# Feed-forward gate and up layers by seven block products instead of eight, from the third pair on, with every remainder taken on GpSimd

## The chip, the core and the metric

The kernel runs on one core of one Trainium2 chip. The metric is device time in microseconds (us), the median of three runs. Only this core is in use. TensorE (PE in the profile) multiplies, ScalarE (ACT) and VectorE (DVE) do elementwise work and read the matmul results out of PSUM, GpSimd (POOL) does elementwise work between SBUF tiles, and SyncE (SP) issues the weight loads.

## What is computed

Four blocks of a network in float32 over a sequence of 512 tokens of width 1024: two layers of mixer, cross attention and feed-forward, then a block with two more mixers and a feed-forward, then a block of three mixers. Three feed-forward layers are in it, all of the same size; the change touches only them.

```python
def _swiglu(h, w_in, w_out):
    a, g = jnp.split(h @ w_in, 2, axis=-1)
    return (jax.nn.silu(a) * g) @ w_out
...
        x = x + _swiglu(_rmsnorm(x, norm_ffn[l]), ffn_w_in[l], ffn_w_out[l])
```

`w_in` has 1024 rows and 2 x 2816 columns, so gate and up are 22 column blocks of 128 each. The first two layers (f0 and f1 below) normalise by a root mean square; the third (fs) has separate gate and up weights and a layer norm ahead of it.

## The kernel before

Activations are kept transposed: 128 partitions are 128 features, the 512 columns are the tokens, and the width of 1024 is 8 tiles. A float32 product is made of three passes of the fast matmul format: each operand is split into a rounded part (high, `XH`, `WH`) and a remainder (low, `XL`, `WL`), and `unit_passes` (L274 to L276) multiplies high by high, high by low and low by high into one PSUM bank.

Weights arrive as a stream of 527 units of 128 x 1024, in an order written out by hand. Each unit passes a pipeline: SP loads it into one of 4 buffers `RW`; ACT rounds it into one of 3 buffers `WH` (`w_hi`, L269), as soon as PE has finished the unit three before; POOL subtracts to get `WL` (L3351); PE multiplies it. One unit of a gate or up layer is one block of 128 output features over all 1024 inputs: 8 weight blocks x 3 passes = 24 matmuls of 512 columns.

The gate and up layer is the class `Pairs`: unit 2i is the gate block i, unit 2i+1 the up block i. PE writes the two into two of four PSUM banks. In f0 and f1 the factor of the root-mean-square norm is applied late, on the result (`late`): DVE multiplies both banks by the factor `NR` (L503, `scaled`), ACT applies Silu to the gate (L488), DVE multiplies the two in SBUF (L525). In fs ACT reads the gate bank itself (L483), and one DVE instruction (L525) multiplies it with the up bank. After 22 pairs comes `Down`, which sums the 22 hidden tiles into all 8 banks; its activations are split by ACT (L638) and DVE (L642). At the start of f0 and f1 DVE makes the remainders of the activations (L936) while PE already works, and at the end of the second unit PE sums squares for the factor, whose reciprocal DVE takes (L976).

Each engine's program is written out in advance and runs in order; engines meet at counting semaphores (`split_hi` and `split_done` for rounded weights and their remainders, `unit_done` for a unit that PE has finished).

## Time and profile before

| | |
|---|---|
| median of three runs | 3389.99 us (3388.49 to 3391.5) |
| profiled execution, first to last instruction | 3388.5 us |
| TensorE's mean granted clock | 0.990 of full speed |
| busy: PE, PEld | 3283.3 us (97%), 2632.3 us (78%) |
| busy: DVE, ACT, POOL | 1319.2, 1220.6, 1331.1 us (39%, 36%, 39%) |
| chain that ended last | PE 86%, DVE 7%, ACT 2% |

The profiled execution lies 1.5 us under the median of the runs. PE is a matmul, PEld its weight load, which overlaps the matmul before it. A matmul's duration in the trace includes its way through the array, so the distance between two starts, not the duration, says what one costs in a row of them.

### The profile page before, as it was taken

The page shows a single profiled execution, that of the slowest core. Times are in us where ns is not written, and L with a number is a line of the kernel's source. Part 1 is how long each engine was busy: PE and PEld are TensorE (multiplying, and loading weights), DVE is VectorE, ACT ScalarE, POOL GpSimd, SP SyncE. Part 2 cuts the span into 40 slices and gives each one's busy share as a digit, 9 for nine tenths or more (in the row PEclk, how much of TensorE's full clock was granted, in tenths as well). Part 3 has the DMA queues.
Part 4 walks back from the last instruction along what each step waited for, and adds up shares of the span by engine and source line. Part 5 has one row for each costly group of instructions (what it writes and reads, how often), then busy time and mean ns, then how long its engine had stood idle before and what let it go on. Part 6 is the DMA issues. An engine that isn't in the chain of part 4 may idle for free.

```text
span 3388.5 us, 41020 instructions
## 1 busy us (share of the span) xinstructions
PE 3283.3 (97%) x17376; PEld 2632.3 (78%) x17376; DVE 1319.2 (39%) x1957; ACT 1220.6 (36%) x1856; POOL 1331.1 (39%) x555
## 2 busy tenths in 40 slices
PE   8999999999999999999999999999899999999998
PEld 6778788887788788886677876888688778878887
DVE  8953421214443421213448652001373261133733
ACT  4543422223343322224434433222335432342332
POOL 5734244443254244443143023444344324415443
PEclk9999999999999999999999999999999999999999
DMA  4222132222232132223123032232232212212332
GB/s 165 87 94 94 50 100 94 99 97 90 69 109 90 56 100 95 98 100 103 49 84 119 19 113 75 99 98 95 81 113 96 72 56 97 90 38 94 100 119 74
DMA packets 83006, 302.48 MB, mean 89 GB/s; under 512 B 9060, under 2 KB 10888, under 8 KB 81928
## 3 DMA queue, kind: packets, MB, share of 16 engines
q1 hardware_dynamic: 78368, 280.55, 25.1%
q10 hardware_dynamic: 4456, 19.33, 1.5%
q8 instruction: 137, 2.24, 0.3%
q14 instruction: 45, 0.37, 0.0%
HBM read 290.39 MB, written 9.44 MB: 88 GB/s over the span
## 4 chain that ended last, share of the span: by engine, by line
PE 86%; DVE 7%; ACT 2%; issue 1%; DVEq 0%; ACTq 0%
PE PS L274 23%; PE PS L276 23%; PE PS L275 23%; PE PS L1197 2%; PE PS L570 2%; PE PS L572 2%; PE PS L571 2%; PE PS L1318 1%; PE PS L2306 1%; DVE XL L936 1%; PE PS L1007 1%; PE PS L2298 1%; PE PS L1183 1%; PE PS L2982 1%; ACT WH L269 0%
## 5 line engine op out<-in xcount | busy, mean ns | idle before, releaser
L3351 POOL TENSOR_TENSOR WL<-RW,WH 128x1024 fp32r<-128x1024 f32 x527 | 1297.3, 2464 | 2029.4 <-ACT WH L269 2028.8
L274 PE MATMUL PS<-XH,WH 128*128 128x512 f32 x2968 | 1169.2, 394 | 33.8 <-DVE XL L936 15.5
L275 PE MATMUL PS<-XL,WH 128*128 128x512 f32 x2968 | 1160.1, 391 | 0.0
L276 PE MATMUL PS<-XH,WL 128*128 128x512 f32 x2968 | 1160.0, 391 | 0.0
L269 ACT ACTIVATE WH<-RW 128x1024 fp32r<-128x1024 f32 x527 | 554.1, 1054 | 802.3 <-PE PS L276 705.7
L274 PEld LDWEIGHTS PS<-XH,WH 128*128 128x128 f32 x2968 | 560.7, 189 | 171.4 <-issue 24.4
L275 PEld LDWEIGHTS PS<-XL,WH 128*128 128x128 f32 x2968 | 560.6, 189 | 117.1 <-issue 2.2
L276 PEld LDWEIGHTS PS<-XH,WL 128*128 128x128 f32 x2968 | 560.2, 189 | 117.4
L274 PE MATMUL PS<-YH,WH 128*128 128x512 f32 (+1 forms) x928 | 349.5, 377 | 7.5 <-DVE A L408 2.9
L276 PE MATMUL PS<-YH,WL 128*128 128x512 f32 (+1 forms) x928 | 348.1, 375 | 0.0
L275 PE MATMUL PS<-YL,WH 128*128 128x512 f32 (+1 forms) x928 | 348.1, 375 | 0.0
L503 DVE TENSOR_TENSOR SG<-PS,NR 128x512 f32<-128x512 f32 x136 | 93.4, 691 | 534.3 <-PE PS L276 533.9
L274 PEld LDWEIGHTS PS<-YH,WH 128*128 128x128 f32 x928 | 175.3, 189 | 42.5 <-POOL WL L3351 6.2
L275 PEld LDWEIGHTS PS<-YL,WH 128*128 128x128 f32 x928 | 175.5, 189 | 31.2
L276 PEld LDWEIGHTS PS<-YH,WL 128*128 128x128 f32 x928 | 175.4, 189 | 31.0
L488 ACT ACTIVATE SG<-SG 128x512 f32<-128x512 f32 x80 | 50.6, 632 | 351.3 <-DVE SG L503 351.2
L642 DVE TENSOR_TENSOR YL<-A,YH 128x512 fp32r<-128x512 f32 x66 | 50.3, 772 | 262.6 <-ACT YH L638 262.6
L408 DVE TENSOR_TENSOR A<-PS,NR 128x512 f32<-128x512 f32 (+1 forms) x84 | 53.3, 638 | 165.1 <-PE PS L276 164.6
L638 ACT ACTIVATE YH<-A 128x512 fp32r<-128x512 f32 x66 | 40.7, 629 | 211.3 <-PE PS L276 211.3
L525 DVE TENSOR_TENSOR A<-SG,PS 128x512 f32<-128x512 f32 x30 | 20.6, 688 | 213.8 <-PE PS L276 202.6
L1241 DVE TENSOR_REDUCE SM<-PS 128x1 f32<-128x256 f32 (+3 forms) x128 | 56.0, 470 | 98.1 <-PE PS L3115 52.2
L1427 DVE SCALAR_TENSOR_TENSOR PS<-A,VEC,PS 128x499 f32<-128x499 f32 (+14 forms) x108 | 79.8, 739 | 4.6 <-ACT A L373 0.8
(549 smaller groups left out, 3089.2 us busy)
## 6 DMA issues: line engine op xcount, KB each, us to landing
RW<-in_units SPq DMA_DIRECT2D x527, 512.0 KB, 3.3
spill<-X ACTq DMA_DIRECT2D x2, 2048.0 KB, 7.5
X<-in_xT SPq DMA_DIRECT2D x8, 256.0 KB, 6.9
A<-spill ACTq DMA_DIRECT2D x1, 2048.0 KB, 8.9
X<-spill ACTq DMA_DIRECT2D x4, 512.0 KB, 5.8
X<-spill ACTq DMA_DIRECT2D x1, 2048.0 KB, 8.6
out_T<-X ACTq DMA_DIRECT2D x4, 512.0 KB, 3.0
spill<-X ACTq DMA_DIRECT2D x1, 1536.0 KB, 5.1
```

What stands on the lines that cost most here:

```text
L269: nc.scalar.activation(WH[:, u % SPLIT, :], RW[:, u % RAW, :], ACT.Copy).then_inc(split_hi, 1)
L274: mm(out, hi, xh, start=first, stop=False)
L275: mm(out, hi, xl, start=False, stop=False)
L276: return mm(out, lo, xh, start=False, stop=last)
L503: st.do(nc.vector.tensor_tensor(dst, bank((e + q) % 4), self.late.r, ALU.mult), name)
L570: mm(o, xh, wh, start=(k == 0), stop=False)
L571: mm(o, xh, wl, start=False, stop=False)
L572: last = mm(o, xl, wh, start=False, stop=(k == KT - 1))
L1197: last = mm(PS[rows, 6 + n % 2, c0:S], value(j), self.pt_of(s, g)[:, j, c0:S], start=(j == 0), stop=(j == (TT if self.keys is None else se ...
L1241: st.do(nc.vector.tensor_reduce(SM[:, c:c + 1], bank(2 * (it % 2) + s, self.blocks_of(it) * P), AX.X, ALU.max, negate=True), f"{self.id}.m ...
L1427: st.do(v.scalar_tensor_tensor(out=y[:, sh:], in0=T(k)[:, :S - sh], scalar=w, in1=y[:, sh:], op0=ALU.mult, op1=ALU.add), f"conv.sum{k}")
L3351: nc.gpsimd.tensor_tensor(WL[:, u % SPLIT, :], RW[:, u % RAW, :], WH[:, u % SPLIT, :].bitcast(F32), ALU.subtract).then_inc(split_done, 1)
```

## The change

From the third pair on, in each of the three layers, the 20 remaining pairs of units are handled by a new class `Sevens`. A pair of units is seen as a 2 x 2 matrix: rows are gate and up, columns are the first and second half of the 1024 inputs. The activations are also seen as 2 x 2: upper and lower half of the inputs by left and right half of the 512 tokens. The eight block products of this 2 x 2 product are replaced by seven (Strassen's method in Winograd's form). Each product has four weight blocks in three passes and 256 columns: 12 matmuls of 256 columns.

The seven left operands (terms, 128 x 512 each) are A11, S1, S2, S4, S3, A12 and A22. Three are halves of the loaded units; the four S are sums of halves, which DVE makes for each pair in advance (`sums`, into `TERM`, `SD`, and S1 over the loaded half itself). Each term is then rounded by ACT (`term_hi`) and its remainder taken by POOL (`pool`). The 3 buffers of `WH` and `WL` become 6 half buffers. Four mixed right operands are made once for each layer (`mix`, `mix_hi`, `mix_lo`), in the time of the first two pairs, which stay as they were. The results are put together in PSUM where it can be done (products S2, S4, S3 and A22 are accumulated onto what stands in a region), and by three copies on ACT and three additions on DVE where it can't.

The counting of the old semaphores is corrected for the units that no longer pass them (`plain`).

```diff
-        A = sb("A", [P, 38, S])
+        with nc.sbuf_tensor("A", [P, 38, S], F32) as A:
+            pass
+        sb("A_LOW", [P, 22, S])
+        MIXED = sb("MIXED", [P, 16, S], F32R)
...
+        def raw_free(eng, u):
+
+            s7 = sevens_of(u)
+            if s7 is None:
+                eng.wait_ge(split_done, plain(u) + 1)
...
+            def gained(self, st, out, half, cols, other, op):
+                if self.gain is None:
+                    st.do(nc.vector.tensor_tensor(out, self.x(half, cols), other, op))
+                else:
+                    for k in range(4):
+                        st.do(nc.vector.scalar_tensor_tensor(out=out[:, k, :], in0=self.x(half, cols)[:, k, :], scalar=vec(self.gain, 4 * half + k),
+                                                             in1=other[:, k, :], op0=ALU.mult, op1=op))
...
+            def mix_hi(self, st, t):
+                st.wait(f"{self.name}.mix{t}")
+                st.do(nc.scalar.activation(self.mixed(t)[0], self.sum_of(t), ACT.Copy), f"{self.name}.mixhi{t}")
+
+            def mix_lo(self, st, t):
+                hi, lo = self.mixed(t)
+                st.wait(f"{self.name}.mixhi{t}")
+                st.do(nc.vector.tensor_tensor(lo, self.sum_of(t), hi.bitcast(F32), ALU.subtract), f"{self.name}.mixed{t}")
+
+            def opening(self, st):
+                for t in range(4):
+                    self.mix(st, t)
+                for t in range(2):
+                    self.mix_lo(st, t)
+
+            def rounded(self, st):
+                for t in range(4):
+                    self.mix_hi(st, t)
+
+            def between(self, st, i):
+                if i == 0:
+                    self.mix_lo(st, 2)
+                    self.sums(st, 0)
+                    self.mix_lo(st, 3)
...
+            def term_hi(self, st, q):
+                p, m = q // 7, q % 7
+                if m in (self.A11, self.A12, self.A22):
+                    raw_landed(st, self.u0 + 2 * p + self.RAWS[m][0])
+                else:
+                    st.wait(f"{self.name}.sum{m}.{p}")
+                if q < 2 * SPLIT:
+                    split_free(st, self.u0 + q // 2)
+                else:
+                    st.wait_ge(product_done, self.base + q - 2 * SPLIT + 1)
+                nc.scalar.activation(WHH[:, self.slot(q), :], self.raw(p, m), ACT.Copy).then_inc(term_hi, 1)
+
+            def pool(self, pool):
+                for q in range(7 * self.n):
+                    w = self.slot(q)
+                    pool.wait_ge(term_hi, self.base + q + 1)
+                    nc.gpsimd.tensor_tensor(WLH[:, w, :], self.raw(q // 7, q % 7), WHH[:, w, :].bitcast(F32), ALU.subtract).then_inc(term_done, 1)
+
+            def sums(self, st, p):
+                a11, a12, a21, a22 = (self.raw(p, m) for m in (self.A11, self.A12, self.S1, self.A22))
+                s2, s3, s4 = (self.raw(p, m) for m in (self.S2, self.S3, self.S4))
+                for w in range(2):
+                    raw_landed(st, self.u0 + 2 * p + w)
+                if p:
+                    st.wait_ge(term_done, self.base + 7 * (p - 1) + self.S3 + 1)
+                st.do(nc.vector.tensor_tensor(s3, a11, a21, ALU.subtract), f"{self.name}.sum{self.S3}.{p}")
+                st.do(nc.vector.scalar_tensor_tensor(out=a21, in0=a21, scalar=-1.0, in1=a22, op0=ALU.mult, op1=ALU.subtract), f"{self.name}.sum{self.S1}.{p}")
+                st.settle()
+                st.do(nc.vector.scalar_tensor_tensor(out=s2, in0=a21, scalar=-1.0, in1=a11, op0=ALU.mult, op1=ALU.subtract), f"{self.name}.sum{self.S2}.{p}")
+                st.settle()
+                st.do(nc.vector.tensor_tensor(s4, a12, s2, ALU.subtract), f"{self.name}.sum{self.S4}.{p}")
...
+                kept = {self.S2: "first", self.S4: "fifth", self.S3: "second", self.A22: "third"}
+                mixes = {self.S1: 0, self.S2: 1, self.S3: 2, self.A22: 3}
+                for p in range(self.n):
+                    for m in range(7):
+                        q = 7 * p + m
+                        st.wait_ge(term_done, self.base + q + 1)
+                        if m == 0:
+                            bank_free(st, self.e0 + 2 * p + 1)
+                        if m in kept:
+                            st.wait(f"{self.name}.{kept[m]}{p}")
+                        if p == 0 and m in mixes:
+                            st.wait(f"{self.name}.mixed{mixes[m]}")
+                        xh, xl = self.operand(m)
+                        for k in range(4):
+                            c = slice(k * P, (k + 1) * P)
+                            last = unit_passes(self.region(p, where[m]), WHH[:, self.slot(q), c], WLH[:, self.slot(q), c], xh[:, k, :], xl[:, k, :],
+                                               k == 0 and m in (self.A11, self.S1, self.A12), k == 3, m in kept)
+                        last.then_inc(product_done, 1)
...
+                    self.done(st, p, 0)
+                    st.do(a.activation(SG[:, j, 0:256], self.region(p, 0), ACT.Copy), f"{self.name}.first{p}")
+                    ahead(0)
+                    self.done(st, p, 1)
+                    st.do(a.activation(SG[:, 2 + j, 256:S], self.region(p, 1), ACT.Copy), f"{self.name}.fifth{p}")
+                    ahead(1)
+                    self.done(st, p, 2)
+                    st.do(a.activation(SG[:, j, 256:S], self.region(p, 0), ACT.Copy), f"{self.name}.second{p}")
+                    for m in range(2, 7):
+                        ahead(m)
+                        if m == 3 and p == self.n - 1:
+                            self.then.lead_act(act, st)
+                    st.wait(f"{self.name}.gated{p}")
+                    st.do(a.activation(SG[:, j, :], SG[:, j, :], self.func), f"{self.name}.func{p}")
...
+                    if p < self.n - 1:
+                        self.sums(st, p + 1)
+                    else:
+                        self.then.lead_dve(dve, st)
+                    self.done(st, p, 3)
+                    st.wait(f"{self.name}.second{p}")
+                    st.do(v_.tensor_tensor(gate[:, right], c, gate[:, right], ALU.add))
+                    self.done(st, p, 4)
+                    st.wait(f"{self.name}.fifth{p}")
+                    st.do(v_.tensor_tensor(up[:, right], a, up[:, right], ALU.add), f"{self.name}.third{p}")
+                    self.done(st, p, 5)
+                    st.wait(f"{self.name}.first{p}")
+                    st.do(v_.tensor_tensor(gate[:, left], b, gate[:, left], ALU.add), f"{self.name}.taken{p}")
+                    st.settle()
+                    if self.late is not None:
+                        st.do(v_.tensor_tensor(gate, gate, self.late.r, ALU.mult), f"{self.name}.gated{p}")
+                        st.do(v_.tensor_tensor(up[:, right], up[:, right], self.late.r[:, right], ALU.mult))
+                    else:
+                        names[f"{self.name}.gated{p}"] = names[f"{self.name}.taken{p}"]
+                    self.done(st, p, 6)
+                    if self.late is not None:
+                        st.do(v_.tensor_tensor(up[:, left], a, self.late.r[:, left], ALU.mult))
+                        st.settle()
+                        st.wait(f"{self.name}.func{p}")
+                        st.do(v_.tensor_tensor(self.dst(self.first + p), gate, up, ALU.mult), f"ev{e + 1}")
+                    else:
+                        st.wait(f"{self.name}.func{p}")
+                        st.do(v_.tensor_tensor(self.dst(self.first + p)[:, left], gate[:, left], a, ALU.mult))
+                        st.do(v_.tensor_tensor(self.dst(self.first + p)[:, right], gate[:, right], up[:, right], ALU.mult), f"ev{e + 1}")
...
-            up = Pairs(f"f{l}.up", NH, at(0), ACT.Silu, ready=f"fn{l}", late=late, first=first)
-            up.then = Down(f"f{l}.down", up, alpha, summed, weights)
-            return up.then
+            up = Pairs(f"f{l}.up", 2, at(0), ACT.Silu, ready=f"fn{l}", late=late, first=first)
+            s7 = up.sevens = Sevens(f"f{l}.up", 2, NH - 2, at(0), ACT.Silu, None if late is None else f"norm_ffn{l}", late, f"fn{l}.biased7")
+            up.opening, up.opening_act, up.rounded, up.between = s7.opening, s7.mix_open_act, s7.rounded, s7.between
+            s7.then = Down(f"f{l}.down", up, alpha, summed, weights)
+            return s7.then
...
+                s7 = sevens_of(u)
+                if s7 is not None:
+                    if u == s7.u0:
+                        s7.pool(pool)
+                    continue
+                pool.wait_ge(split_hi, plain(u) + 1)
```

The instruction order of DVE shows what a pair is made of. This is DVE in f0, before, from the reciprocal of the norm's factor on (names in front of `<-` are written, behind it read; `SG` is the working tile of a pair, `A` on the left of L525 the hidden tile):

```order
L976 RECIPROCAL NR<-NR 128x512
L503 TENSOR_TENSOR SG<-PS,NR 128x512 x2
L525 TENSOR_TENSOR A<-SG 128x512
L503 TENSOR_TENSOR SG<-PS,NR 128x512 x2
L525 TENSOR_TENSOR A<-SG 128x512
```

In the changed kernel the same place reads (L679 are the four mixes in 16 pieces, L711 their remainders, L552 and L576 the old pair, L763 to L768 the sums):

```order
L1251 RECIPROCAL NR<-NR 128x512
L679 SCALAR_TENSOR_TENSOR A<-X,VEC,A 128x256 x16
L711 TENSOR_TENSOR MIXED<-A,MIXED 128x1024 x2
L552 TENSOR_TENSOR SG<-PS,NR 128x512 x2
L576 TENSOR_TENSOR A<-SG 128x512
L711 TENSOR_TENSOR MIXED<-A,MIXED 128x1024
L763 TENSOR_TENSOR TERM<-RW 128x512
L764 SCALAR_TENSOR_TENSOR RW<-RW 128x512
L766 SCALAR_TENSOR_TENSOR SD<-RW 128x512
L768 TENSOR_TENSOR TERM<-RW,SD 128x512
L711 TENSOR_TENSOR MIXED<-A,MIXED 128x1024
```

The mixes and two of their remainders stand ahead of the first pair's own three instructions, and the other two remainders with the first sums ahead of the second pair's. From then on a pair of `Sevens` in f0 and f1 is these eleven DVE instructions (the sums are those of the next pair):

```order
L763 TENSOR_TENSOR TERM<-RW 128x512
L764 SCALAR_TENSOR_TENSOR RW<-RW 128x512
L766 SCALAR_TENSOR_TENSOR SD<-RW 128x512
L768 TENSOR_TENSOR TERM<-RW,SD 128x512
L844 TENSOR_TENSOR SG<-PS,SG 128x256
L847 TENSOR_TENSOR SG<-PS,SG 128x256
L850 TENSOR_TENSOR SG<-PS,SG 128x256
L853 TENSOR_TENSOR SG<-SG,NR 128x512
L854 TENSOR_TENSOR SG<-SG,NR 128x256
L859 TENSOR_TENSOR SG<-PS,NR 128x256
L862 TENSOR_TENSOR A<-SG 128x512
```

Three instructions have become eleven, and the four sums stand ahead of the additions that PE's last product of the pair waits for (L847, named `third`). On POOL the order before ends, after a few taps of a convolution (L1408, L1410) between the first units, in one instruction for each of the other 505 units:

```order
L1410 TENSOR_TENSOR A<-A 128x501 [waits pool_taps]
L3351 TENSOR_TENSOR WL<-RW,WH 128x1024 [waits split_hi]
L1408 TENSOR_SCALAR A<-A,VEC 128x500 [waits pool_taps]
L1410 TENSOR_TENSOR A<-A 128x500 [waits pool_taps]
L3351 TENSOR_TENSOR WL<-RW,WH 128x1024 [waits split_hi] x505
```

and POOL's order in the changed kernel at f0 has the following in its place, seven of half the width for each pair:

```order
L3633 TENSOR_TENSOR WL<-RW,WH 128x1024 [waits split_hi] x46
L754 TENSOR_TENSOR WL<-RW,WH 128x512 [waits term_hi] x2
L754 TENSOR_TENSOR WL<-SD,WH 128x512 [waits term_hi]
L754 TENSOR_TENSOR WL<-TERM,WH 128x512 [waits term_hi] x2
L754 TENSOR_TENSOR WL<-RW,WH 128x512 [waits term_hi] x4
L754 TENSOR_TENSOR WL<-SD,WH 128x512 [waits term_hi]
```

Two instructions of 1024 columns for each pair have become seven of 512.

## Rows read from the trace of the kernel before

**Rows 1.** The page, part 1: busy time, share, instructions of each engine

```profile
PE 3283.3 (97%) x17376; PEld 2632.3 (78%) x17376; DVE 1319.2 (39%) x1957; ACT 1220.6 (36%) x1856; POOL 1331.1 (39%) x555
```

**Rows 2.** Busy time in stretches of f0 and fs, then clock, DMA share

```profile
440.00:640.00 200.00, 200.00 (x884) 165.68 (x883) 38.67 (x56) 48.65 (x55) 90.48 (x38) 1.00 0.30 99
2100.00:2300.00 200.00, 200.00 (x884) 165.68 (x883) 12.38 (x18) 48.48 (x56) 86.91 (x37) 1.00 0.30 98
```

**Rows 3.** Timeline of DVE in f0: start, duration, engine, line, what, idle before

```profile
499.77 0.69 DVE L503 TENSOR_TENSOR SG<-PS,NR 128x512 f32<-128x512 f32 x1 [4.02 <-PE PS L276]
505.21 0.69 DVE L503 TENSOR_TENSOR SG<-PS,NR 128x512 f32<-128x512 f32 x1 [4.75 <-PE PS L276]
505.94 0.69 DVE L525 TENSOR_TENSOR A<-SG 128x512 f32<-128x512 f32 x1
510.65 0.69 DVE L503 TENSOR_TENSOR SG<-PS,NR 128x512 f32<-128x512 f32 x1 [4.02 <-PE PS L276]
```

**Rows 4.** Timelines of ACT and POOL at the same place of f0

```profile
500.50 0.63 ACT L488 ACTIVATE SG<-SG 128x512 f32<-128x512 f32 x1 [5.04 <-DVE SG L503]
501.03 1.04 ACT L269 ACTIVATE WH<-RW 128x1024 fp32r<-128x1024 f32 x1
...
502.15 2.40 POOL L3351 TENSOR_TENSOR WL<-RW,WH 128x1024 fp32r<-128x1024 f32 x1 [4.16 <-ACT WH L269]
506.41 2.47 POOL L3351 TENSOR_TENSOR WL<-RW,WH 128x1024 fp32r<-128x1024 f32 x1 [1.85 <-ACT WH L269]
```

**Rows 5.** Timeline of PE in the memory keys, 21 steps of 256 columns

```profile
156.26 0.28 PE L276 MATMUL PS<-YH,WL 128*128 128x256 f32 x1
...
158.78 0.28 PE L276 MATMUL PS<-YH,WL 128*128 128x256 f32 x1
```

**Rows 6.** Timeline of POOL, 501 beside 1024 columns, and two in a row

```profile
127.89 1.27 POOL L1410 TENSOR_TENSOR A<-A 128x501 f32<-128x501 f32 x1
129.12 2.40 POOL L3351 TENSOR_TENSOR WL<-RW,WH 128x1024 fp32r<-128x1024 f32 x1
...
435.69 4.76 POOL L3351 TENSOR_TENSOR WL<-RW,WH 128x1024 fp32r<-128x1024 f32 x2 [9.06 <-ACT WH L269]
```

**Rows 7.** Timelines of POOL and DVE where both have work in a row

```profile
962.00 26.86 POOL L3351 TENSOR_TENSOR WL<-RW,WH 128x1024 fp32r<-128x1024 f32 x10 [1.41 <-ACT WH L269]
...
962.47 2.49 DVE L895 TENSOR_TENSOR XL<-A,XH 128x512 fp32r<-128x512 f32 x1 [0.44 <-ACT XH L1852]
964.88 0.41 DVE L408 TENSOR_TENSOR A<-PS,NR 128x256 f32<-128x256 f32 x1
965.22 2.56 DVE L895 TENSOR_TENSOR XL<-A,XH 128x512 fp32r<-128x512 f32 x1
...
979.31 2.56 DVE L895 TENSOR_TENSOR XL<-A,XH 128x512 fp32r<-128x512 f32 x1
```

**Rows 8.** Timeline of DVE at the start of f0; last row, 2048 columns

```profile
413.91 4.38 DVE L936 SCALAR_TENSOR_TENSOR XL<-X,VEC,XH 128x512 fp32r<-128x512 f32 x4 [0.87 <-ACT XH L926]
...
418.80 2.74 DVE L936 SCALAR_TENSOR_TENSOR XL<-X,VEC,XH 128x512 fp32r<-128x512 f32 x4
...
429.81 3.35 DVE L976 RECIPROCAL NR<-NR 128x512 f32<-128x512 f32 x1 [5.44 <-ACT NR L968]
...
439.93 0.69 DVE L503 TENSOR_TENSOR SG<-PS,NR 128x512 f32<-128x512 f32 x1 [3.88 <-PE PS L276]
...
147.48 2.28 DVE L1514 TENSOR_TENSOR A<-A 128x2048 f32<-128x2048 f32 x1
```

**Rows 9.** Timeline of DVE at the end of f0's pairs

```profile
654.95 4.28 DVE L642 TENSOR_TENSOR YL<-A,YH 128x512 fp32r<-128x512 f32 x4 [2.17 <-ACT YH L638]
...
659.87 2.17 DVE L525 TENSOR_TENSOR A<-SG 128x512 f32<-128x512 f32 x1
```

**Rows 10.** Timeline of DVE at the start of fs

```profile
2080.45 0.69 DVE L895 TENSOR_TENSOR XL<-X,XH 128x512 fp32r<-128x512 f32 x1 [0.59 <-ACT XH L1054]
2086.80 0.69 DVE L525 TENSOR_TENSOR A<-SG,PS 128x512 f32<-128x512 f32 x1 [5.65 <-ACT SG L483]
```

More of the change, by code:

```diff
@@ L260, in bank_free, with sevens_of, plain, raw_landed @@
                 st.wait_ge(*reached(f"ev{e - 4}"))
+        SEVENS = []
+        def sevens_of(u):
+            for s7 in SEVENS:
+                if s7.u0 <= u < s7.u0 + 2 * s7.n:
+                    return s7
+            return None
+        def plain(u):
+            return u - sum(min(max(u - s7.u0, 0), 2 * s7.n) for s7 in SEVENS)
+        def raw_landed(st, u):
+            st.wait_ge(raw_full[u % RAW], 16 * (u // RAW + 1))
+        def raw_free(eng, u):
[3 more added lines that the diff above has]
+            else:
+                eng.wait_ge(term_done, s7.base + 7 * ((u - s7.u0) // 2) + 6 + (u - s7.u0) % 2)
+        def split_free(st, u):
+            if u >= SPLIT:
+                s7 = sevens_of(u - SPLIT)
+                if s7 is None:
+                    st.wait_ge(unit_done, plain(u - SPLIT) + 1)
+                else:
+                    st.wait_ge(product_done, s7.base + 7 * s7.n - 6 + 2 * (u - s7.u0 - 2 * s7.n + 1))
         def w_hi(act, st, v):
@@ L265, in w_hi, with unit_passes @@
                 u = st.unit
-                st.wait_ge(raw_full[u % RAW], 16 * (u // RAW + 1))
-                if u >= SPLIT:
-                    st.wait_ge(unit_done, u - SPLIT + 1)
-                nc.scalar.activation(WH[:, u % SPLIT, :], RW[:, u % RAW, :], ACT.Copy).then_inc(split_hi, 1)
+                s7 = sevens_of(u)
+                if s7 is not None:
+                    if u - s7.u0 >= SPLIT:
+                        return
+                    for q in range(2):
+                        s7.term_hi(st, 2 * (u - s7.u0) + q)
+                else:
+                    raw_landed(st, u)
+                    split_free(st, u)
+                    nc.scalar.activation(WH[:, u % SPLIT, :], RW[:, u % RAW, :], ACT.Copy).then_inc(split_hi, 1)
                 st.unit = u + 1
-        def unit_passes(out, hi, lo, xh, xl, first, last):
-            mm(out, hi, xh, start=first, stop=False)
-            mm(out, hi, xl, start=False, stop=False)
-            return mm(out, lo, xh, start=False, stop=last)
+        def unit_passes(out, hi, lo, xh, xl, first, last, onto=False):
+            mm(out, hi, xh, start=first, stop=False, skip_group_check=onto)
+            mm(out, hi, xl, start=False, stop=False, skip_group_check=onto)
+            return mm(out, lo, xh, start=False, stop=last, skip_group_check=onto)
         def pe_tile(pe, st, u, e, xh, xl, cols):
-            st.wait_ge(split_done, u + 1)
+            st.wait_ge(split_done, plain(u + 1))
             bank_free(st, e)
@@ L440, in __init__ @@
             def __init__(self, name, n, dst, func, of=0, yh=None, acc=False, ready=None, u_off=0, func2=None, late=None, first=1,
-                         between=None, between_act=None, between_pe=None, eager=0):
+                         between=None, between_act=None, between_pe=None, eager=0, opening=None, opening_act=None, rounded=None):
                 self.eager, self.held = eager, False
+                self.opening, self.opening_act, self.rounded = opening, opening_act, rounded
                 self.between, self.between_act, self.between_pe = between, between_act, between_pe
@@ L473, in scalar @@
                     w_hi(act, st, self.u0 + SPLIT - 1)
+                if self.opening_act is not None:
+                    self.opening_act(st)
                 if self.opens():
@@ L476, in scalar @@
                     self.late.rstd_act(act, st)
+                if self.rounded is not None:
+                    self.rounded(st)
                 for i in range(self.n):
@@ L509, in vector @@
                 drained(st, self.e0)
+                if self.opening is not None:
+                    self.opening(st)
                 for i in range(self.n):
@@ L617, in tensor @@
                 for k in range(NH - 2):
-                    st.wait_ge(split_done, u0 + k + 1)
+                    st.wait_ge(split_done, plain(u0 + k + 1))
                     st.wait_ge(*reached(f"{self.name}.lo{k}"))
                     for j in (4, 5, 6, 7, 0, 1, 2, 3):
+                        if k == 0 and j >= 6:
+                            st.wait(f"{self.up.sevens.name}.taken{self.up.sevens.n - 8 + j}")
                         if k == 0 and j < 4:
@@ L1998, in gate_pe @@
             u = gate_unit(r) + n
-            st.wait_ge(split_done, u + 1)
+            st.wait_ge(split_done, plain(u + 1))
             for k in range(KT):
```

137 lines of the change are left out of this document (109 added, 28 removed).

## The prediction

> **What bounds the kernel now.** I read the page's busy times first: PE is busy 97% of the span [rows 1], so PE looks like the bound. Its busy share is an overlap of pipelined matmuls, so I went to stretches inside the layers that change: in 200 us of f0 and 200 us of fs PE has no gap at all, while POOL is busy 90.48 and 86.91 us, DVE 38.67 and 12.38, ACT 48.65 and 48.48 [rows 2]. Here PE alone sets the pace. The timeline gives that pace: DVE is released by the end of each unit, at 499.77, 505.21 and 510.65, so a unit takes 5.44 us and a pair 10.88 [rows 3]; that is 48 matmuls of 512 columns at 0.227 us.
>
> The same view shows what a pair leaves on the other engines: DVE three instructions of 0.69 [rows 3]; ACT one Silu of 0.63 and two roundings of 1.04; POOL two remainders of 2.40 and 2.47 [rows 4].
>
> **PE's side of the change.** A row of 256-column matmuls stands in the memory keys: 21 steps in 158.78 - 156.26 = 2.52 us, 0.120 each [rows 5]. That this is so near half of 0.227 says the weight load hides there too. A new pair has 7 x 4 x 3 = 84 of them: 10.08 us. So if PE stays the bound, a pair gains 0.80 us and 60 pairs gain 48 us. The saving is 7%, not an eighth, because the half-width step costs 0.120 and not 0.1135.
>
> **POOL's side.** Seven remainders of 512 columns take the place of two of 1024. A 501-column subtraction-like instruction starts 1.23 us ahead of the next; two of 1024 in a row take 4.76, the second 2.40 of it, a step of 2.36 [rows 6]. The slope is 1.13 us over 523 columns, so 512 columns cost 1.23 + 0.02 = 1.25 in a row. Seven: 8.8 us. That alone still fits under 10.08.
>
> **Where the two meet.** It doesn't fit together with DVE. Where both engines have a queue of work, ten POOL remainders take 26.86 us in place of 10 x 2.36 = 23.6, and seven DVE subtractions with both inputs in SBUF (L895, from 962.47 to 979.31, the first and last shown) take 2.49 to 2.57 us in place of 0.69 [rows 7]. They alternate one to one: DVE waits until POOL's instruction ends, POOL then waits for DVE's. One DVE instruction costs POOL (26.86 - 23.6) / 7 = 0.47 us. Between them stands an addition-like instruction of 256 columns that reads PSUM, at its 0.41 undisturbed [rows 7]. The three-operand form is held up the same way: four took 4.38 beside POOL, 2.74 without [rows 8]. In the loop of before this never matters: POOL rests 5.4 - 2.4 us in each unit, and the one meeting shows as 2.47 in place of 2.40 [rows 4].
>
> The Trainium skill, "SBUF — State Buffer", section "SBUF: two separate sides", says the same as a rule: GpSimd and a VectorE instruction with two SBUF inputs take a shared port pair exclusively, for the whole instruction. By that rule the sum would be durations added whole, 7 x 1.25 + 6 x 0.69 + 0.42 = 13.3 us for a pair of f0; by the rows, where start-up is hidden, it is less, and I go by the rows.
>
> Of the eleven DVE instructions of a pair in f0 and f1, seven read two SBUF tiles: four sums, the gate by the factor, the product (512 columns, 0.47 each) and the right half of up by the factor (256 columns; 0.69 - 0.41 = 0.28 shorter, so 0.20). POOL's queue then takes 8.8 + 6 x 0.47 + 0.20 = 11.8 us for a pair. In fs there is no factor, and the final product reads PSUM on its left half: 8.8 + 4 x 0.47 + 0.20 = 10.9 us.
>
> **DVE's order.** DVE isn't short of time by its own durations (4 + 2 of 0.69, and 0.42 five times: 6.2 us), but it runs in order, and PE's seventh product accumulates onto a region that DVE must have read (`third`), which stands behind the four sums. I laid out a pair with POOL always at work. The four sums take 4 x (1.25 + 0.47) = 6.9 us. The three additions from PSUM take 1.14 (0.42, then two at a step of 0.36) under POOL's fifth instruction; `third` is done at 7.7. Then gate by factor, 8.7 at its end; right half, 10.2; left half from PSUM, 10.6; product, after POOL's seventh, 11.9. PE's seventh product runs from 7.7 to 9.2 and gives free the half buffers that POOL's next terms need, in time. So both queues close at 11.8 to 11.9 us. One place is a tie: the gate's instruction is ready at about the moment POOL takes its sixth (8.1). If POOL wins it, DVE waits 1.25 more, and the pair takes 13.1. I take 12.1: the closed schedule, with 0.2 for ties now and then. In fs the chain is 6.9 + 1.14, then ScalarE's rounding and Silu behind PE's seventh product (9.2 + 0.63 + 0.63 = 10.5), 0.42 and 0.3 more: 11.2, against 10.9 for POOL. I take 11.1.
>
> ACT: seven roundings of 512 columns at the 0.63 that Silu of that width takes [rows 4], three copies of 256 columns, which I put at DVE's 0.42, Silu 0.63: 6.3 us in all. It is hidden under PE's pair of 12; without that cover it would still end before POOL. SP loads the same bytes, and gets its buffers back when POOL has passed A12 and A22, most of a pair ahead of their next reader; no cost.
>
> **The openings.** In f0 and f1 the mixes stand behind the reciprocal, which ends at 433.2 [rows 8]. PE finishes the two old pairs at 439.9 (the release of L503 there). By then DVE has to do 16 pieces of 256 columns (four of 512 in a row take 2.74 [rows 8], a step of 0.68, less 0.28 for the half width: 0.41 each, 6.6 us, with four waits for the one before at 0.1: 440.3), two remainders of 1024 columns (2048 take 2.28, 512 take 0.69, so 1.2 each), to 442.7, and only then the first old pair. The first term is rounded by ACT behind that pair's Silu, 444.6; POOL ends at 445.9, and PE stands 6 us. Then the third remainder, the first sums and the fourth remainder keep DVE until 452, the second old pair until 454, and terms S2 and S4 are queued on ACT behind its Silu: 455. DVE makes the next sums until 461 and `third` at 462; the first new pair ends at 463.4. That is 23.5 us after 439.9, or 11.5 over a pair of 12. In fs no factor is awaited: activations are complete at 2081.1, the first pair's product is asked for at 2086.8 [rows 10], DVE needs 4 x 1.2 + 2 x 1.2 = 7.2; ACT's fourth unit is late by about 1.5.
>
> **The ends.** In the last pair four remainders for the down layer stand where the sums stood. Before, four took 4.28 us beside POOL and the product 2.17 [rows 9], without a gap on PE. Now PE's seventh product waits behind them, and POOL has the down layer's units of 2.4 in the same stretch: from 0 to 6 us, I take 3 for each of three layers.
>
> **The sum.** f0 and f1: 40 x (12.1 - 10.88) = 49. fs: 20 x (11.1 - 10.88) = 4. Openings 2 x 11.5 + 1.5 = 24.5. Ends 9. Together +87 on the profiled 3388.5, 3475; the median of the runs lies 1.5 above it: 3477 us, 2.6% slower.
>
> **Rivals.** *A, DVE loses the ties.* Each of the seven waits for a full POOL instruction; 13.1 in f0 and f1, 11.6 in fs: 89 + 14 + 24.5 + 12 = +140, 3530 us. For it: every one of the seven in rows 7 did wait in full. Against: POOL then has idle time, and DVE meets it free. Chance 0.22.
>
> *B, POOL loses less.* Meetings fall into POOL's own waits for rounded terms, pairs take 11.2 and 10.8: 13 - 2 + 20 + 4 = +35, 3425 us. For it: a meeting cost only 0.07 where POOL had slack [rows 4]. Against: POOL has slack only if it isn't the bound. Chance 0.15.
>
> *C, faster.* The port matters little for half-width instructions, and PE stays the bound at 10.08. It decides once POOL and its meetings take less than 10.08, that is under 0.2 us for each meeting in f0. Then -48 + 24.5 + 4 = -20, 3370 us. For it: 8.8 alone does fit. Against: the 0.47 of rows 7, seven times without exception. Chance 0.08.
>
> *D, TensorE's clock.* PE rests about 2 us in each pair. In full work the granted clock is 1.00, the 2.4 GHz level [rows 2], and the page of before has 0.990 over a span with longer rests than these, so I don't expect the 1.2 GHz level; if it fell, a pair would need 168 half steps, 20 us, and the time would pass 3700. Chance 0.03.
>
> **How the numbers follow.** The forecast has 0.50, A 0.22, B 0.15, C 0.08, D 0.03, and 0.02 is for no change. A difference under 0.2% can't be told from none here. The cases slower than that are the forecast, A, B and D: 0.89 to 0.90, less a little of B that lies near nothing. Faster 0.08, same 0.04, slower 0.88. The range leaves out D, C and the thin ends of A and B: 3415 to 3545. The likeliest case alone would be 3450 to 3500.
>
> **What would show it.** POOL busy nearly throughout f0's pairs, its 512-column instructions at 1.3 when alone and about 1.7 behind a DVE instruction; DVE's sums at 1.5 to 1.8 us in place of 0.69; a pair at 12 us in f0 and f1 and 11 in fs; PE busy in steps of 0.120 with a wait ahead of the product behind `third`; a gap of about 6 us on PE where the third pair of f0 begins. I am wrong if POOL's instructions stay at 1.3 while DVE's sums run, or if PE shows no gaps between products.

## The result and the profile after

The changed kernel takes 3477.45 us (median of four runs, 3474.64 to 3486.56) against 3390.74 (3388.49 to 3392.55). The ratio is 1.0263, 95% interval 1.0248 to 1.0279: slower by 2.6%. The profiled execution has a span of 3472.8 us, 84.3 more than before.

The page of the kernel after, part 1 and the first line of part 4 (the chain that ended last), beside [rows 1]:

```profile
PE 3266.2 (94%) x19536; PEld 2716.0 (78%) x19536; DVE 1859.0 (54%) x2485; ACT 1423.5 (41%) x2356; POOL 1695.3 (49%) x855
PE 71%; DVE 16%; ACT 4%; issue 4%; POOL 1%; DVEq 0%; ACTq 0%
```

PE's busy time falls by only 17 us, since matmuls overlap, and its share of the chain falls from 86 to 71%: it now waits. Stretches of f0 and fs show where, in the columns of [rows 2]:

```profile
440.00:640.00 200.00, 170.81 (x1333) 167.84 (x1332) 189.31 (x183) 96.52 (x182) 184.13 (x115) 0.95 0.26 85
2180.00:2300.00 120.00, 111.28 (x909) 109.55 (x910) 88.42 (x96) 61.81 (x119) 105.18 (x76) 1.00 0.30 96
```

In f0, where PE had no gap, it is busy 171 of 200 us, and POOL is busy 184 where it was 90. The timelines of DVE and then POOL through one settled pair of f0 show the alternation of [rows 7] on every remainder:

```profile
563.40 1.78 DVE L763 TENSOR_TENSOR TERM<-RW 128x512 f32<-128x512 f32 x1
565.10 1.78 DVE L764 SCALAR_TENSOR_TENSOR RW<-RW 128x512 f32<-128x512 f32 x1
566.91 1.67 DVE L766 SCALAR_TENSOR_TENSOR SD<-RW 128x512 f32<-128x512 f32 x1
568.62 1.67 DVE L768 TENSOR_TENSOR TERM<-RW,SD 128x512 f32<-128x512 f32 x1
570.21 0.41 DVE L844 TENSOR_TENSOR SG<-PS,SG 128x256 f32<-128x256 f32 x1
570.54 0.41 DVE L847 TENSOR_TENSOR SG<-PS,SG 128x256 f32<-128x256 f32 x1
...
571.32 0.69 DVE L853 TENSOR_TENSOR SG<-SG,NR 128x512 f32<-128x512 f32 x1
571.92 1.52 DVE L854 TENSOR_TENSOR SG<-SG,NR 128x256 f32<-128x256 f32 x1
...
562.89 6.85 POOL L754 TENSOR_TENSOR WL<-RW,WH 128x512 fp32r<-128x512 f32 x4
569.70 1.72 POOL L754 TENSOR_TENSOR WL<-SD,WH 128x512 fp32r<-128x512 f32 x1
571.38 3.21 POOL L754 TENSOR_TENSOR WL<-TERM,WH 128x512 fp32r<-128x512 f32 x2
```

The sums take 1.67 to 1.78 us in place of 0.69, the additions that read PSUM their own 0.41. POOL never rests in it. L853 at 0.69 is the tie of the prediction, won by DVE. On PE the seventh product waits for L847 (`third`) in each pair:

```profile
664.43 0.35 PE L318 MATMUL PS<-MIXED,WH 128*128 128x256 f32 x1 [1.36 <-DVE SG L847]
676.10 0.35 PE L318 MATMUL PS<-MIXED,WH 128*128 128x256 f32 x1 [1.36 <-DVE SG L847]
```

676.10 - 664.43 = 11.67 us a pair. By the starts of the first matmul of each pair, and without the first and the last one, f0 has 11.72 on average (11.4 to 11.6 and 12.1 to 12.2 in turn from the second to the seventh, then 11.67), f1 11.67 and fs 11.18.

From the first matmul of its gate and up layer to the first of its down layer, f0 lost 33.9 us, f1 32.7 and fs 12.9. The other 4.9 lie outside these stretches.

### The profile page after: what moved, and what is told of

Its sections match the earlier page's. It is cut to its first block, busy times and chain, and to the rows that moved or that the text cites. A ratio compares the mean times of both kernels' runs of the same rounds, so it can differ in the third digit from the quotient of the medians.

```text
span 3472.8 us, 46965 instructions
## 1 busy us (share of the span) xinstructions
PE 3266.2 (94%) x19536; PEld 2716.0 (78%) x19536; DVE 1859.0 (54%) x2485; ACT 1423.5 (41%) x2356; POOL 1695.3 (49%) x855
## 4 chain that ended last, share of the span: by engine, by line
PE 71%; DVE 16%; ACT 4%; issue 4%; POOL 1%; DVEq 0%; ACTq 0%
PE PS L318 19%; PE PS L320 18%; PE PS L319 18%; DVE TERM L763 2%; DVE RW L764 2%; DVE SD L766 2%; PE PS L1472 2%; PE PS L621 2%; PE PS L623 2%; PE PS L622 2%; PE PS L2583 1%; ACT WH L748 1%; PE PS L1593 1%; DVE XL L1211 1%; DVE SG L844 1%
## 5 line engine op out<-in xcount | busy, mean ns | idle before, releaser
L3633 POOL TENSOR_TENSOR WL<-RW,WH 128x1024 fp32r<-128x1024 f32 x407 | 1006.6, 2477 | 1668.7 <-ACT WH L313 1668.1
L318 PE MATMUL PS<-XH,WH 128*128 128x512 f32 (+1 forms) x2728 | 1004.3, 368 | 47.2 <-DVE XL L1211 15.3
L319 PE MATMUL PS<-XL,WH 128*128 128x512 f32 (+1 forms) x2728 | 994.8, 365 | 0.0
L320 PE MATMUL PS<-XH,WL 128*128 128x512 f32 (+1 forms) x2728 | 994.0, 364 | 0.0
L313 ACT ACTIVATE WH<-RW 128x1024 fp32r<-128x1024 f32 x407 | 427.0, 1053 | 589.0 <-PE PS L320 492.4
L754 POOL TENSOR_TENSOR WL<-RW,WH 128x512 fp32r<-128x512 f32 x240 | 381.0, 1605 | 72.1 <-ACT WH L748 70.4
L318 PE MATMUL PS<-YH,WH 128*128 128x512 f32 (+1 forms) x928 | 350.6, 378 | 17.5 <-POOL WL L3633 12.6
L318 PE MATMUL PS<-MIXED,WH 128*128 128x256 f32 x960 | 278.6, 290 | 75.2 <-DVE SG L847 66.3
L320 PE MATMUL PS<-MIXED,WL 128*128 128x256 f32 x960 | 273.5, 285 | 0.0
L319 PE MATMUL PS<-MIXED,WH 128*128 128x256 f32 x960 | 273.5, 285 | 0.0
L318 PEld LDWEIGHTS PS<-MIXED,WH 128*128 128x128 f32 x960 | 185.7, 193 | 86.1 <-issue 75.7
L748 ACT ACTIVATE WH<-RW 128x512 fp32r<-128x512 f32 x240 | 150.5, 627 | 157.3 <-DVE RW L764 82.3
L319 PEld LDWEIGHTS PS<-MIXED,WH 128*128 128x128 f32 x960 | 186.1, 194 | 0.0
```

The source lines that it names most:

```text
L313: nc.scalar.activation(WH[:, u % SPLIT, :], RW[:, u % RAW, :], ACT.Copy).then_inc(split_hi, 1)
L318: mm(out, hi, xh, start=first, stop=False, skip_group_check=onto)
L319: mm(out, hi, xl, start=False, stop=False, skip_group_check=onto)
L320: return mm(out, lo, xh, start=False, stop=last, skip_group_check=onto)
L748: nc.scalar.activation(WHH[:, self.slot(q), :], self.raw(p, m), ACT.Copy).then_inc(term_hi, 1)
L754: nc.gpsimd.tensor_tensor(WLH[:, w, :], self.raw(q // 7, q % 7), WHH[:, w, :].bitcast(F32), ALU.subtract).then_inc(term_done, 1)
```

## The experiments

Ten kernels, each timed against the kernel before in the same batch (3389.7, 3390.2 and 3389.8 us). They build on the changed kernel, where nothing else is said.

### 1. Fewer DVE instructions that read two SBUF tiles

The gate is put together in a free PSUM bank, and up in the unused half of the bank of region 1; the down layer waits for those banks. In f0 and f1 the DVE instructions of a pair that read two SBUF tiles fall from 7 to 4, in fs from 5 to 4; their number and widths stay.

```diff
-st.do(v_.tensor_tensor(gate[:, right], c, gate[:, right], ALU.add))
+st.do(v_.tensor_tensor(gate_p[:, right], c, gate[:, right], ALU.add))
...
-st.do(v_.tensor_tensor(gate, gate, self.late.r, ALU.mult), f"{self.name}.gated{p}")
+st.do(v_.tensor_tensor(gate, gate_p, self.late.r, ALU.mult), f"{self.name}.gated{p}")
```

> The gate and the right half of up are kept in PSUM between their steps instead of in SBUF; same instructions, same order, same widths. Of the eleven DVE instructions of a pair in f0 and f1, those with two SBUF inputs fall from 7 to 4. Port theory: POOL's queue needs 8.8 + 4 x 0.47 = 10.7 us, the chain over the seventh product and Silu then rules as it does in fs, a pair of f0 and f1 falls from 11.7 to about 11.2, fs stays at 11.2, the time is about 3457 us. Rival (the number and order of DVE's instructions, whatever they read): nothing changes, 11.7 a pair, 3477 us.

Measured: 3428.23 us, ratio 1.0112 [1.0096, 1.0129]; pairs of 10.58 in all three layers. The port theory holds, and the gain is more than I gave it, because the chain that was to hold the pairs at 11.2 didn't: fs fell too. There the right half of the product takes 0.41 us in place of 1.05 and the first sum behind it 1.02 in place of 1.79, and POOL is busy 119.6 of 120 us (2180 to 2300), where it was 105.2. A stretch of f0, in the same columns as above:

```profile
500.00:640.00 140.00, 136.40 (x1115) 134.14 (x1114) 121.77 (x146) 76.73 (x147) 139.53 (x93) 1.00 0.30 99
```

POOL is busy 139.5 of 140 us: a pair is POOL's queue, 8.8 + 4 x 0.445. The same price comes out of f0 of the changed kernel, (11.67 - 8.8) / 6.5 = 0.44.

### 2. Half of each remainder

POOL's remainders take 256 columns in place of 512 from the seventh term on. This leaves out the other half of each remainder; DVE's and PE's work is whole.

```diff
-nc.gpsimd.tensor_tensor(WLH[:, w, :], self.raw(q // 7, q % 7), WHH[:, w, :].bitcast(F32), ALU.subtract).then_inc(term_done, 1)
+h = slice(0, S) if q < 2 * SPLIT else slice(0, 256)
+nc.gpsimd.tensor_tensor(WLH[:, w, h], self.raw(q // 7, q % 7)[:, h], WHH[:, w, h].bitcast(F32), ALU.subtract).then_inc(term_done, 1)
```

> Leaves out half of each remainder: POOL's instructions in the new class are 256 columns wide instead of 512 (from the seventh on), all else stays. POOL then needs 7 x 0.7 = 4.9 us a pair and 8.1 with the meetings. Port theory: PE is the bound, a pair takes 84 x 0.120 = 10.1 to 10.3 us in all three layers, about 3397 us. Rival 1 (PE pays for its waits ahead of each product): pairs stay above 10.6, over 3420 us. Rival 2 (DVE's order alone): f0 and f1 stay near 11.7.

Measured: 3394.79 us, ratio 1.0015 [1.0006, 1.0024]; every pair 10.08 us in all three layers. So PE could do a pair in the 84 x 0.120 of the prediction, which gains 0.80 on each, some 46 us over the 57 distances between new pairs; but it ends 5 us above the kernel before. Openings and ends cost 42 us of their own, even with POOL at leisure (the first new pair of f0 and f1 still takes 19.1), and 8 us lie outside the three layers.

### 3. Mixes ahead of the reciprocal

```diff
+if self.opening is not None:
+    drained(st, self.e0)
+    self.opening(st, range(4), ())
 if self.opens():
     self.late.rstd_dve(dve, st)
```

> The four mixes are moved ahead of the reciprocal on DVE, into the 5.4 us in which it waits for ScalarE; their remainders stay behind it. If the opening is what the in-order DVE makes of it, each of f0 and f1 gains 3 to 4 us, the third pair of f0 starts near 442 instead of 445.6, and the time is about 3470 us. Rival (ScalarE's rounding of the mixes and its table load set the start): nothing or under 1 us a layer, 3476 us.

Measured: 3478.73 us (3471.5 to 3483.86), ratio 1.0262 [1.0246, 1.0277]: no gain in the median. In the profiled execution the 16 mixes took 8.82 us beside POOL's units in place of 6.70, and pushed the reciprocal to 435.1; the first new pair began at 443.9 in place of 445.6. PE had begun f0 1.65 us later, though: from its first unit there to the first new pair it is 25.6 us in f0 and in f1, in place of 29.0. So each opening is 3.4 shorter, as expected, but the time doesn't show it: 7 us in all is within the spread of the runs (12 us).

### 4. The down layer's units earlier

`ahead` was meant to round the down layer's first units during the last pair, but `w_hi` returns at once there, because its count still stands inside the new class. The edit sets it (and places one wait of the down layer anew, for the last pair's bank):

```diff
 elif m in (2, 4):
+    st.unit = max(st.unit, self.u0 + 2 * self.n)
     w_hi(act, st, self.u0 + 2 * self.n + m // 2 - 1)
```

> The first two units of the down layer are rounded during the last pair, as the code intends; in the changed kernel they are rounded only after the last Silu, and PE waits 3.65 us for POOL. If that wait is what the end costs, the gap before the down layer closes and 2 to 3 us a layer come back, 3469 us. Rival: POOL, which then has 2.4 us instructions beside DVE's four remainders in the last pair, holds up the seventh product by as much, 3477 us.

Measured: 3490.05 us, ratio 1.0297 [1.0281, 1.0312]: 12 us slower. It is the rival's mechanism, and it costs more than the rival's 3477. End of f0, timelines of DVE, POOL and PE:

```profile
689.13 6.44 DVE L918 TENSOR_TENSOR YL<-A,YH 128x512 fp32r<-128x512 f32 x4 [5.37 <-ACT YH L914]
...
688.66 2.41 POOL L3634 TENSOR_TENSOR WL<-RW,WH 128x1024 fp32r<-128x1024 f32 x1 [2.09 <-ACT WH L313]
691.68 2.73 POOL L3634 TENSOR_TENSOR WL<-RW,WH 128x1024 fp32r<-128x1024 f32 x1 [0.62 <-ACT WH L313]
...
696.38 0.55 PE L318 MATMUL PS<-MIXED,WH 128*128 128x256 f32 x1 [4.85 <-DVE SG L848]
```

And the windows from the end of that rest on:

```profile
696.00:700.00 4.00, 3.62 (x15) 3.46 (x16) 2.24 (x6) 1.25 (x2) 0.00 (x0) 0.50 0.22 83
```

The hidden tiles' remainders start 2.2 us later in the pair, since its first product ran slowly and ACT rounds the down layer's first unit ahead of the hidden tiles; then they meet 2.4 us instructions and take 6.44 in place of 2.50. `third` stands behind them, PE rests 4.85, and the granted clock is then 0.50, the 1.2 GHz level: the last product takes 2.9 us in place of 1.7. The last pairs take 17.6, 16.4 and 16.4 us in place of 14.1, 14.1 and 13.5, which is 8.6 of the 12. Besides, f0's pairs stayed at 11.3 and 12.5 in turn to its end, 11.91 on average, where the changed kernel settled at 11.67. The edit doesn't touch those pairs, so this part isn't shown to be its doing.

### 5. S4 behind `third`

```diff
 st.do(v_.tensor_tensor(up[:, right], a, up[:, right], ALU.add), f"{self.name}.third{p}")
+if p < self.n - 1:
+    self.sum4(st, p + 1)
```

> The changed kernel with one DVE instruction moved in all three layers: the sum S4 of the next pair stands behind the addition that the seventh product waits for (third), no longer ahead of it; nothing added or removed. If POOL's 7 remainders and DVE's port instructions bound f0 and f1 (port theory: POOL is busy 100% there), their pairs stay at 11.6 to 11.7 us; fs, where POOL idles 1.3 us a pair, may fall from 11.17 towards 10.9: 3472 to 3477. If the order of DVE is the bound (the seventh product waits 1.36 us for third, which comes 1.7 us earlier now), pairs fall to 10.3 in f0 and f1 and 10.1 in fs: 3400 to 3405.

Measured: 3463.08 us, ratio 1.0215 [1.02, 1.0231], 14 less. f0 and f1 stay at 11.63, as the port theory has it; fs falls from 11.17 to 10.75, further than expected (the time was to be 3472 to 3477), and POOL is busy 100.00 of 100 us there too (2180 to 2280): 8.8 + 4.5 x 0.43. The rest comes from the first new pair, 19.1 and 19.6 in place of 21.0 and 20.8. So fs was bound by the order of DVE, f0 and f1 by POOL.

### 6. A spread opening

Four old pairs in f0 and f1, and one piece of the making-ready behind each.

```diff
+if i == 0:
+    for t in range(4):
+        self.mix(st, t)
+elif i == 1:
+    for t in range(4):
+        self.mix_lo(st, t)
+elif i == 2:
+    self.sums(st, 0)
```

> The changed kernel, with four old pairs instead of two ahead of the new ones in f0 and f1, and the making of the mixed operands and of the first sums spread behind each of them (mixes behind pair 0, their remainders behind pair 1, sums behind pair 2); fs as it was. If the opening's 15.6 us (start 5.5 late, first new pair 21.0 instead of 10.9) come from DVE's crowded list, the first new pair starts without delay and takes 12 to 13 us, and with two pairs of 10.88 in place of 11.7 each of f0 and f1 is 14 to 16 us shorter: 3445 to 3449. If the long first pair lies in the way the new pairs start (half buffers, TERM waiting for POOL), only the late start and the two cheap pairs are won: 3462 to 3466. If the mixes beside POOL's 2.4 us instructions cost more than they did beside none, PE waits inside the old pairs, and the gain is under 10 us: 3468 or more.

Measured: 3452.88 us, ratio 1.0187 [1.0173, 1.0201], 25 less, between the two cases. The new pairs begin at 463.0, where PE is free, but the first takes 17.0 us in f0 and 15.8 in f1. PE's waits in f0's first new pair:

```profile
465.08 0.39 PE L318 MATMUL PS<-MIXED,WH 128*128 128x256 f32 x1 [0.47 <-POOL WL L771]
468.30 0.35 PE L318 MATMUL PS<-MIXED,WH 128*128 128x256 f32 x1 [1.52 <-ACT SG L832]
477.34 0.55 PE L318 MATMUL PS<-MIXED,WH 128*128 128x256 f32 x1 [3.07 <-DVE SG L864]
```

The 16 mixes took 13.1 us between POOL's 2.4 us instructions, so the first sums ended at 465.5 and the second ones, which wait for POOL to release TERM, at 476.5, with `third` behind them.

### 7. One remainder on DVE

On kernel 1: A22's remainder is taken by DVE, and S4 stands behind `third`.

```diff
 st.do(nc.vector.scalar_tensor_tensor(out=a21, in0=a21, scalar=-1.0, in1=a22, op0=ALU.mult, op1=ALU.subtract), f"{self.name}.sum{self.S1}.{p}")
+if low:
+    self.low(st, p - 1)
...
+if q % 7 == 6 and self.on_dve:
+    continue
```

> The gate-in-PSUM kernel (3428, pairs 10.58 in all layers) with the remainder of A22 taken by DVE, 6 left on POOL, and S4 behind third. POOL would need 6 x 1.25 + 5 x 0.47 = 9.85 us a pair, below PE's 10.08. If POOL's time alone decides, pairs are 10.1 in all layers: 3400. If each DVE port instruction takes its turn behind one of POOL's (mean 1.55 us for the four sums now), DVE needs some 11.3 us a pair in f0 and f1 and 10.0 in fs: fs 10.1 (9 us won), f0 and f1 11.3 (28 lost): 3445 to 3450. A miss of both: f0 and f1 at 10.58, 3419.

Measured: 3400.78 us, ratio 1.003 [1.0019, 1.0041]; pairs of 10.2 in all three layers. The first case held, the turn-taking rival fell: with POOL at rest in between, DVE meets it free. A stretch of f0:

```profile
520.00:620.00 100.00, 100.00 (x825) 99.18 (x824) 85.49 (x119) 55.25 (x107) 87.07 (x59) 1.00 0.31 106
```

Timelines of DVE and POOL in it:

```profile
562.39 0.68 DVE L771 TENSOR_TENSOR WL<-RW,WH 128x512 fp32r<-128x512 f32 x1
563.10 0.69 DVE L785 SCALAR_TENSOR_TENSOR SD<-RW 128x512 f32<-128x512 f32 x1
...
563.21 1.73 POOL L766 TENSOR_TENSOR WL<-RW,WH 128x512 fp32r<-128x512 f32 x1 [1.29 <-ACT WH L758]
```

### 8. Kernel 1 with the spread opening and repaired ends

The ends are those of experiment 4, with only the first of the four hidden remainders ahead of the last pair's additions.

```diff
-self.then.lead_dve(dve, st)
+self.then.lo(dve, st, 0)
```

> The gate-in-PSUM kernel with the spread opening, and at each layer's end the down layer's units rounded and split during the last pair, with only the first of DVE's four hidden remainders ahead of the last pair's additions. Pairs 10.58. Opening 15 us less in f0 and f1 each, less 0.6 for two pairs of 10.88; ends 3 us less in all three: 3428 - 29 - 9 = 3390, 3385 to 3395, no difference from the kernel before. If the long first pair is inherent: 3408. If POOL's 2.4 us instructions at the end again hold DVE up by more than they save: 3399 to 3405.

Measured: 3396.56 us, ratio 1.0017 [1.0009, 1.0026]. From the start of f0's last pair to the down layer it is 11.2 us (646.3 to 657.5), 0.6 over a pair, where the changed kernel had 14.1, 2.4 over one. What it missed of 3390 (3385 to 3395) is the first new pair, 15.9 and 17.1.

### 9. All together

Kernel 7 with the ends of 8, and four old pairs in all layers; two mixes stand ahead of the reciprocal, where DVE was idle, two behind pair 0, the first sums behind pair 1 already, two mixed remainders behind pair 2.

```diff
+elif i == 1:
+    for t in (0, 1):
+        self.mix_lo(st, t)
+    self.sums(st, 0)
+    self.sum4(st, 0)
```

> The gate-in-PSUM kernel with the remainder of A22 on DVE and S4 behind third (pairs 10.2 by the run before), the ends of the run before it (0.7 us each), and in all three layers four old pairs ahead of the new ones, with two mixes ahead of the reciprocal in f0 and f1, the first sums behind pair 1 and the last mixed remainders behind pair 2. A layer then has 18 new pairs, 17 of them 10.2 instead of 10.88: -11.6. If the openings were only a matter of order, the first new pair starts without delay and takes 11.5: +0.6, end +0.7: -10.2 a layer, 3360 in all, the first version faster than before by over 0.5%. If the start of the new class costs what it did (first pair 15.9 in f0 and f1, fs late by 5): -6 a layer, 3371.

Measured: 3359.91 us (3358.76 to 3360.96), ratio 0.9912 [0.9896, 0.9929]: faster than the kernel before by 0.9%, as worked out. The first new pair takes 10.98, 10.98 and 10.33. In the whole opening of f0, 441 to 475 us, PE has one wait:

```profile
471.46 0.36 PE L321 MATMUL PS<-MIXED,WH 128*128 128x256 f32 x1 [0.68 <-DVE PS L895]
```

### 10. Two remainders on DVE

Against kernel 9, which leaves to DVE the remainders from `per` on:

```diff
-                self.per = 6
+                self.per = 5
```

> The kernel beside it in this batch with A12's remainder on DVE too (5 on POOL, 2 on DVE). POOL: 5 x 1.25 + 6 x 0.47 = 9.1 us a pair, with room. If PE's 10.08 is then all that bounds, pairs are 10.08 instead of 10.2: 6 us below that kernel. If DVE is the next bound (busy 8.7 us a pair with one remainder in f0 and f1, and 0.7 to 1.7 more with the second), its pairs are 10.3 to 10.4 in f0 and f1 and 10.08 in fs: 2 to 5 us above that kernel.

Measured: 3359.43 us, ratio 0.9912 [0.9897, 0.9927]: no different from kernel 9. Pairs take 10.24 in all three layers, not 10.08 and not 10.4. POOL is busy 74.65 of 100 us in f0 and no longer matters, DVE is at 92.52; the 0.16 over 10.08 lies about the seventh product (starts 7.2, 8.73 and 10.24 in a pair). Which hand-over sets it wasn't tested.

## Why the prediction was right

**The time** came out on the forecast, 3477.45 against 3477, because terms that were too high made up for terms that were too low; that it came this near is luck. By the starts of pairs and down layers in the profiled executions (us over before):

| term | forecast | measured |
|---|---|---|
| 40 pairs of f0 and f1 | 49 | 32 |
| 20 pairs of fs | 4 | 6 |
| openings of f0, f1 | 23 | 30 |
| opening of fs | 1.5 | 5 |
| ends | 9 | 7 |
| elsewhere | 0 | 5 |

The stretches outside the three layers differ by several us from kernel to kernel (the one from f0's down layer to f1's first unit by 4). What the 5 us are stays open.

**PE's side** held exactly: 10.08 a pair in experiment 2, once it is not kept waiting.

**POOL and the port**: the cause is shown from both sides, by taking work from POOL (2, 7), and by leaving the work and taking away only the second SBUF operand (1). Adding durations whole, as the rule of the Trainium skill ("SBUF — State Buffer", section "SBUF: two separate sides") would have it, gives 13.3, and f0 measured 11.67; by the price of 0.47 it was 11.8. The price measured is 0.43 to 0.45 in three kernels, with POOL's own work at the 8.8 of the prediction. A pair of f0 and f1 came to 11.67 where the sum had 12.1: of the term of 49, 17 us too much. The closed schedule of 11.8 was near; the 0.2 for ties and 0.03 of the price were the excess.

**The tie** (rival A) is real. In the changed kernel's first pairs and in all of experiment 4's f0 it is lost in every other pair, and the pair that follows takes 12.1 to 12.6. Once it is won twice in a row, it is won for good. The rows put it down to TensorE's clock:

```profile
500.44 0.42 DVE L850 TENSOR_TENSOR SG<-PS,SG 128x256 f32<-128x256 f32 x1 [0.32 <-PE PS L320]
500.90 1.50 DVE L853 TENSOR_TENSOR SG<-SG,NR 128x512 f32<-128x512 f32 x1
...
512.34 0.36 PE L318 MATMUL PS<-MIXED,WH 128*128 128x256 f32 x1 [1.77 <-DVE SG L847]
```

And the windows from 490 (a pair starts at 490.22) and about the rest of 1.77:

```profile
490.00:494.00 4.00, 4.00 (x23) 4.00 (x22) 3.58 (x4) 2.05 (x4) 3.79 (x4) 0.58 0.00 0
512.00:516.00 4.00, 3.66 (x23) 3.69 (x24) 3.67 (x6) 1.87 (x4) 4.00 (x4) 0.73 0.02 4
```

At the granted clock of 0.58 the pair's second product starts 2.56 us behind its first, in place of 1.44. The sixth product ends late, L850 waits 0.32 for it, L853 comes just behind POOL and takes 1.50, the next `third` is late, and PE rests 1.77 ahead of the seventh product. Behind that rest the clock is low again, in the pair after. Each lost tie of f0 in the changed kernel (3) and in experiment 4 (9) has this wait of L850 and this slow first product; between the first and the last pair, no tie that was won has either. The one rest of 1.80 that left the clock at 1.00 (536 to 540) ended the alternation, and in f1, where PE rests 0.93 in the first new pair in place of 2.12, it never began. So the chain is read from the rows; no experiment changed the clock alone.

The pairs never came to A's 13.1 throughout, because a pair that loses it leaves POOL a rest of 1.30 us, and DVE meets it free in the next. **B** had pairs of 11.2 in f0, that is 0.37 for a meeting, and it is 0.44. **C** needed POOL's queue under 10.08: it took experiments 7 and 9 to get there, and then the sign did turn.

**fs**: a pair took 11.17, forecast 11.1, and the chain through the four sums was the reason, as experiment 5 shows. The opening of fs is the step that failed: 1.5 in the sum, 4.6 measured. PE at the fourth unit:

```profile
2162.88 0.79 PE L318 MATMUL PS<-XH,WH 128*128 128x512 f32 x1 [2.75 <-POOL WL L3633]
```

And a window behind it:

```profile
2163.00:2167.00 4.00, 4.00 (x12) 3.21 (x13) 3.93 (x4) 1.64 (x3) 2.71 (x2) 0.64 0.36 133
```

ACT rounds the fourth unit only at 2158.66, behind four mixed roundings and a table load of 1.28. PE rests 2.75 and then runs at a granted clock of 0.64.

**The openings of f0 and f1**: the start was forecast at 446 and came at 445.6, the end of the first new pair at 463.4 and came at 466.6. The step that I left out is a wait of DVE: the second sums overwrite TERM, and POOL must first have read S3 of the first.

```profile
457.35 1.65 DVE L763 TENSOR_TENSOR TERM<-RW 128x512 f32<-128x512 f32 x1 [3.74 <-POOL WL L754]
...
464.89 0.36 PE L318 MATMUL PS<-MIXED,WH 128*128 128x256 f32 x1 [2.12 <-DVE SG L847]
```

**The clock** (rival D) did fall, but only behind the rests of the openings and ends and behind the rests of 1.77 us above: 0.77 from 440 to 470, 0.93 from 470 to 520, against 1.00 from 520 to 680. It is part of the openings' cost; a product at the start of f0 takes 2.9 us there. The prediction, which put rests of 2 us in each pair at nothing for the clock, was right by the settled rest of 1.36, not by its reason.

**The ends** measured 14.1 - 11.7 = 2.4 for f0, forecast 3, by another mechanism. I had POOL take the down layer's units beside the last pair; in truth they were rounded only after the last Silu, and PE waited for the first:

```profile
688.16 2.93 ACT L313 ACTIVATE WH<-RW 128x1024 fp32r<-128x1024 f32 x3
...
689.28 7.01 POOL L3633 TENSOR_TENSOR WL<-RW,WH 128x1024 fp32r<-128x1024 f32 x3 [6.73 <-ACT WH L313]
...
691.68 0.79 PE L318 MATMUL PS<-YH,WH 128*128 128x512 f32 x1 [3.64 <-POOL WL L3633]
```

What I had assumed is experiment 4, and there it costs more, not less: 5.7 us over a pair in f0, 4.7 and 5.2 in the others.

**Where the 48 us went**: the faster product is there in full, but POOL's queue cost 83 (3477.5 against 3394.8 with half remainders), openings and ends 45 (by experiment 2, with all 60 pairs at 10.08), and 8 lie outside the three layers. With the port relieved, one remainder moved, the ends repaired and the openings put in order, 30 of the 48 are kept, with 54 new pairs in place of 60.

## What to carry over

When a change swaps matrix work for elementwise work, lay the new pair out as a queue on each engine, and price each meeting of GpSimd with a VectorE instruction that reads two SBUF tiles (here 0.44 us on GpSimd's queue, up to 1.1 on VectorE's); moving one operand to PSUM takes the meeting away at no cost. Put an instruction that another engine waits for ahead of work that is only made ready for later. A class that starts three times costs its opening three times: spread it behind work that leaves the engine idle, and check the first of a series for buffers that the last one still holds. Look at the granted clock in windows of a few us: behind a short rest it can cost a product of the next pair, and a stretch of 50 us shows only 0.93.

## What the runs showed of the hardware

- A VectorE instruction that reads one tile from SBUF and one from PSUM kept its 0.41 (256 columns) or 0.69 (512) beside a busy GpSimd, also where it writes PSUM. I had expected less of it than 49 us.
- Two engines that meet in a loop of fixed work settled in either of two rhythms, 11.67 us a pair, or 11.3 and 12.5 in turn. The four runs of the changed kernel lie up to 12 us apart; whether the rhythm is the cause isn't shown. In the second rhythm the granted clock was 0.93 (470 to 520 us, changed kernel) and 0.91 to 0.96 (520 to 680, experiment 4), in the first 1.00. Rests of TensorE, a low clock for the product behind them and a lost tie follow one another there.
- Behind rests of TensorE of 4.85 and 2.75 us the granted clock was 0.50 and 0.64 over four us. Of the 12 rests of 1.77 to 1.80 us in f0's pairs of the changed kernel and experiment 4, 11 were followed by a slow product; rests of 1.36 us in every settled pair of f0 left the clock at 1.00.
